# Attention probabilities gated before the transpose, values as stationary weights, modulation rows through DRAM, and channel sums on VectorE, in a decoder layer on one core

## The reference

```python
mod = silu(c) @ w_ada + b_ada                       # six vectors of 1024
h = rmsnorm(x, g_pre_mix) * (1 + sc1) + sh1
q, k_c, k_s, k_w, v_c, v_s, v_w, g_nsa, glu, g_merge = split(h @ w_in)
# 16 heads in 4 groups of 4; q and k 96 wide, v 64 wide
o = g[0] * softmax(q kc') vc + g[1] * softmax(q ks' + bias) vs + g[2] * softmax(q kw' + bias) vw
y_b = silu(layernorm(depthwise_conv31(a * sigmoid(gate)))) @ w_conv_out
y = sigmoid(g_a) * (o @ w_attn_out) + sigmoid(g_b) * y_b
x = x + gt1 * rmsnorm(y @ w_out, g_post_mix)
h = rmsnorm(x, g_pre_ffn) * (1 + sc2) + sh2
# product-key retrieval: 8 heads x top-16 of 16384 experts for each token
x = x + gt2 * rmsnorm(sum_e coef_e * v[e], g_post_ffn)
```

## Time and profile before

| | us |
|---|---|
| Median of 3 runs | 1219.2 |
| Lowest and highest | 1200.63, 1225.37 |
| Profiled execution | 1195.33 |
| Its span, first to last instruction | 1193.6 |
| TensorE matmul busy in the span | 1004.1 (84%) |
| VectorE busy | 728.4 (61%) |
| ScalarE busy | 278.1 (23%) |
| GpSimd busy | 324.7 (27%) |

### The profile page before, as it was taken

How to read it: one execution, slowest core, us unless ns; L and a number is a source line. 1 busy time by engine, 2 the same in 40 slices (tenths; PEclk the granted TensorE clock), 3 DMA queues, 4 the chain that set the end, 5 groups by cost and what they waited for, 6 DMA issues and landing times.

```text
span 1193.6 us, 10994 instructions
## 1 busy us (share of the span) xinstructions
PE 1004.1 (84%) x3386; PEld 617.0 (52%) x3386; DVE 728.4 (61%) x1772; ACT 278.1 (23%) x731; POOL 324.7 (27%) x311
## 2 busy tenths in 40 slices
PE   5899999999999996969888777788777777778676
PEld 5688888787667763845453333333333332333222
DVE  6699895222646313465547676777677767666553
ACT  3111122231535202231212221222132212221211
POOL 0201000010000000224335644444544444445420
PEclk9899999999959998989998989988998989989998
DMA  9977648838000232498788999999999999999992
GB/s 370 403 302 227 245 159 319 298 96 186 1 1 2 92 137 88 155 423 327 303 335 331 425 422 423 423 423 424 422 422 424 423 421 424 422 424 422 422 425 121
DMA packets 62536, 361.37 MB, mean 303 GB/s; under 512 B 7275, under 2 KB 7915, under 8 KB 29452
## 3 DMA queue, kind: packets, MB, share of 16 engines
q0 software_dynamic: 42400, 290.47, 60.4%
q1 hardware_dynamic: 20076, 70.18, 16.7%
HBM read 359.05 MB, written 1.57 MB: 302 GB/s over the span
## 4 chain that ended last, share of the span: by engine, by line
PE 49%; DMA 36%; DVE 5%; ACT 3%; issue 2%; POOL 2%; SPq 2%; POOLq 0%; ACTq 0%; DVEq 0%
DMA arena<-in_peer_uv,idx 33%; PE pb L423 21%; PE pb L649 13%; PE pb L454 4%; PE pb L575 2%; DMA ring<-in_w_stream 2%; PE pb L547 2%; POOL qT L396 2%; DVE arena L1205 1%; PE pb L474 1%; DMA hT<-in_peer_uv,idx 1%; PE pb L558 1%; PE pb L571 1%; ACT sig L845 1%; PE pb L530 1%
## 5 line engine op out<-in xcount | busy, mean ns | idle before, releaser
L649 PE MATMUL pb<-arena,sig 128*128 128x512 f32 x444 | 222.9, 651 | 62.4 <-ACT sig L845 62.4
L396 POOL DMA_INDIRECT arena<-in_peer_uv,idx x111 | 127.1, 1145 | 263.9 <-PE pb L649 137.6
L423 PE MATMUL pb<-hT,ring 128*128 128x256 f32 x880 | 190.7, 379 | 1.2 <-ACT hT L801 0.7
L1205 DVE CUSTOM_DVE_ANT_0 arena<-arena,sig 128x1024 f32<-128x1024 f32 x111 | 135.0, 1227 | 90.5 <-DMA arena<-in_peer_uv,idx 90.1
L649 PEld LDWEIGHTS pb<-arena,sig 128*128 128x128 f32 x444 | 91.2, 210 | 185.4 <-issue 185.4
L423 PEld LDWEIGHTS pb<-hT,ring 128*128 128x128 f32 x880 | 167.0, 190 | 25.2 <-ACT arena L708 1.7
L649 PE MATMUL pb<-ring,sig 128*128 128x512 f32 x208 | 110.0, 689 | 37.0 <-ACT sig L845 37.0
L840 ACT ACTIVATE gl<-dot 128x4 f32<-128x4 f32 x64 | 13.1, 205 | 407.7 <-DVE dot L1205 407.6
L649 PEld LDWEIGHTS pb<-ring,sig 128*128 128x128 f32 x208 | 45.0, 222 | 101.9 <-issue 101.9
L947 DVE SCALAR_TENSOR_TENSOR y<-arena,cols,y x240 | 95.2, 483 | 0.0
L845 ACT ACTIVATE sig<-ident,cf 128x128 f32<-128x128 f32 x256 | 81.8, 390 | 18.3 <-DVE cf L1211 18.3
(11 more groups left out here) (221 smaller groups left out, 1335.7 us busy)
## 6 DMA issues: line engine op xcount, KB each, us to landing
ring<-in_w_stream SPq DMA_DIRECT2D x103, 512.0 KB, 4.7
arena<-in_w_ada POOLq DMA_DIRECT2D x32, 512.0 KB, 9.9
arena<-in_w_ada SPq DMA_DIRECT2D x12, 512.0 KB, 13.1
arena<-in_w1k SPq DMA_DIRECT2D x8, 512.0 KB, 6.0
sig<-in_w_ada SPq DMA_DIRECT2D x4, 512.0 KB, 15.2
arena<-in_w1v POOLq DMA_DIRECT2D x1, 2048.0 KB, 8.1
arena<-rev_scratch POOLq DMA_DIRECT2D x8, 256.0 KB, 11.0
arena<-in_peer_uv,idx POOLq DMA_INDIRECT x111, 25.8
```

The costliest lines, as they stand in the source:

```text
L396: nc.gpsimd.indirect_dma_start(out=rowat[PLACE[n]], out_offset=None, in_=a["peer_uv"], in_offset=bass.IndirectOffsetOnAxis(ap=idx[:, c, e: ...
L423: last = mm(pb[:, bank, 0:SEQ], w[:, k * P:(k + 1) * P], src[:, k, :], start=(k == 0), stop=(k == DT - 1))
L649: last = mm(pb[:, 4 + 2 * t + hf, :], diag[:, c % DEEP, e, :], rowat[PLACE[n]][:, D + hf * 512:D + (hf + 1) * 512], start=(i == 0 and e == ...
L1205: V_.tensor_tensor_reduce(out=u, in0=u, in1=h2[:, c // CPT, :], scale=1.0, scalar=0.0, op0=ALU.mult, op1=ALU.add, accum_out=dot[:, c % DEE ...
```

## The change

1. *Gating.* VectorE multiplies reciprocal sums and gates for each unit (`shares`), and scales the exponentials in `S` before their transposition (`gated`, one `tensor_scalar` for each of two branches); for the compressed branch `cmp_gated` does this once a group. Transposes wait for that. `S` has four buffers now, in `y`'s place.
2. *Values.* `values` is done once a group: V (128 keys x 64) is the stationary operand, the probabilities of four heads (512 columns) the moving one, and all branches accumulate in one bank. The result is transposed already: ScalarE copies it to `hT` (`attention_out`). `combine`, `attn` and its transposes are gone. TensorE, ScalarE and VectorE run their steps in another order (below).
3. *Scores* of the first token tile are computed for its 128 keys only.
4. *Rows.* TensorE transposes `vec4` ahead of the V projections, ScalarE copies it to `vrow`, GpSimd writes it to DRAM, and reads each row back to all partitions by a broadcast DMA, three after the subkeys and one after the last values. `row` and `wide` are gone. `T_OUT` products go tile by tile with the merge (`v_m`), into banks 2 to 5.
5. *Channel sums.* VectorE adds the eight tiles, and TensorE multiplies `ones` once with the sum. The mean stands ahead of the V projections, the variance ahead of the `w1k` block.

Cut to its core:

```diff
         S_ = pair[:, 0:D]
-        S = S_.rearrange("p (u b t) -> p u b t", u=2, b=2)
+        S = yf.rearrange("p (u b t) -> p u b t", u=4, b=2)
         revsb = pair[0:HEADS, 0:512]
-        wide = S_.rearrange("p (j t) -> p j t", j=DT)
         junk = sc[:, 0:1024]
         tmp = pair[:, D:2 * D]
-        PT = tmp.rearrange("p (a b) -> p a b", a=2)
+        PT = arena[:, 8:12, :].rearrange("p a b -> p (a b)").rearrange("p (u k t) -> p u k t", u=2, t=512)
         scaled = [tmp, sc[:, 1024:2048]]
         spare = sb("spare", [P, 2 * D])
-        PcT = spare[:, 0:512]
+        PcT = spare[:, 1024:2048].rearrange("p (u t) -> p u t", u=2)
...
+            g.wait_ge(a_vec, 1)
+            g.dma_start(rows_dram, vrow[:, :]).then_inc(rows_out, 16)
             g.wait_ge(p_hk, 1)
             g.dma_start(w1[:, 0:CMP_ST, :], a["w1v"]).then_inc(w1v_in, 16)
...
             g.dma_start(subk, a["subkeys"]).then_inc(sub_in, 16)
+            g.wait_ge(rows_out, 16)
+            for v in range(4):
+                if v == 3:
+                    g.wait_ge(p_o, GROUPS * TT)
+                g.dma_start(rows[v], rows_dram[v * DT:(v + 1) * DT].rearrange("j p -> (j p)").partition_broadcast(P)
+                            ).then_inc(rows_in, 16)
...
+            pe.wait_ge(v_vec, 4)
+            nc.tensor.transpose(pb[0:4 * DT, 7, 256:256 + P], vec4[:, :, :].rearrange("p v j -> p (v j)"),
+                                ident[:, :]).then_inc(p_vec, 1)
+            pe.wait_ge(v_ys, 1)
+            mm(pb[:, 4, 0:SEQ], ones[:, :], tmp[:, 0:SEQ], start=True, stop=True).then_inc(p_mean, 1)
             pe.wait_ge(a_evac, evacuated(T_V - 1))
             for k in range(DT):
                 token_tile(k, T_V + k, hT, (0, 2), VHALF)
 
 
-            pe.wait_ge(v_y, 2)
-            for k in range(DT):
-                last = mm(pb[:, 4, 0:SEQ], ones[:, :], y[:, k, :], start=(k == 0), stop=(k == DT - 1))
-            last.then_inc(p_mean, 1)
-
+            pe.wait_ge(v_sq, 1)
+            mm(pb[:, 4, SEQ:2 * SEQ], ones[:, :], tmp[:, SEQ:2 * SEQ], start=True, stop=True).then_inc(p_var, 1)
 
             pe.wait_ge(w1_in, 128)
             pe.wait_ge(v_pos, 4)
...
-                pe.wait_ge(a_cexp, gi + 1)
+                pe.wait_ge(v_pc, gi + 1)
...
-                mm(pb[:, n % 2, :], qT[0:DQK, h, tt * P:(tt + 1) * P], kT[0:DQK, g, 1:3, :],
+                mm(pb[:, n % 2, 0:2 * keys], qT[0:DQK, h, tt * P:(tt + 1) * P], kT[0:DQK, g, 1:3, 0:keys],
                    start=True, stop=True).then_inc(p_s, 1)
...
-                pe.wait_ge(a_exp, 2 * (n + 1))
+                pe.wait_ge(v_p, 2 * (n + 1))
...
-            def values(n):
-                tt, h, g, hh, keys = unit_keys(n)
-                gi = n // REP
-                pe.wait_ge(a_pt, n + 1)
+            def values(gi):
+                tt, g = group_of(gi)
                 pe.wait_ge(a_pct, gi + 1)
-                if gi >= 1 and hh % 2 == 0:
-                    pe.wait_ge(v_o, 2 * (gi - 1) + hh // 2 + 1)
-                o = (hh % 2) * 3 * DV
-                bank = 6 + hh // 2
-                mm(pb[:, bank, o:o + DV], PcT[0:NCMP, hh * P:(hh + 1) * P], vcv[:, g * DV:(g + 1) * DV],
-                   start=True, stop=True)
+                pe.wait_ge(a_pt, REP * (gi + 1))
+                if gi >= 2:
+                    pe.wait_ge(a_o, 2 * (gi - 1))
+                o = pb[0:DV, 6 + gi % 2, :]
+                mm(o, vcv[:, g * DV:(g + 1) * DV], PcT[0:NCMP, gi % 2, :], start=True, stop=False)
                 for b in range(2):
                     for kb in range(tt + 1):
-                        last = mm(pb[:, bank, o + (1 + b) * DV:o + (2 + b) * DV],
-                                  PT[:, n % 2, (b * (tt + 1) + kb) * P:(b * (tt + 1) + kb + 1) * P],
-                                  V[:, kb, (b * GROUPS + g) * DV:(b * GROUPS + g + 1) * DV],
-                                  start=(kb == 0), stop=(kb == tt))
+                        last = mm(o, V[:, kb, (b * GROUPS + g) * DV:(b * GROUPS + g + 1) * DV],
+                                  PT[:, gi % 2, b * (tt + 1) + kb, :], start=False, stop=(b == 1 and kb == tt))
                 last.then_inc(p_o, 1)
 
-            for n in range(NU + 2):
+            for n in range(NU + 3):
                 if n < NU:
                     if n % REP == 0:
                         cmp_scores(n // REP)
                     scores(n)
-                    if n % REP == 1:
+                    if n % REP == 2:
                         cmp_transposes(n // REP)
-                if 1 <= n <= NU:
-                    transposes(n - 1)
-                if n >= 2:
-                    values(n - 2)
-
-
-            pe.wait_ge(v_at, 2 * GROUPS * TT)
+                if 2 <= n < NU + 2:
+                    transposes(n - 2)
+                if n >= REP + 2 and (n - 3) % REP == REP - 1:
+                    values((n - 3) // REP)
+
+
             pe.wait_ge(a_pt, NU)
             pe.wait_ge(a_pct, GROUPS * TT)
-            for t in range(TT):
-                for jj in range(2):
-                    for j in range(4):
-                        last = nc.tensor.transpose(pb[:, 2 + 2 * t + jj, j * P:(j + 1) * P],
-                                                   attn[:, t, (4 * jj + j) * P:(4 * jj + j + 1) * P], ident[:, :])
-                    last.then_inc(p_at, 1)
 
             wide_bank = (0, 1, 6, 7)
 
-            pe.wait_ge(a_xT, 4)
-            pe.wait_ge(v_o, 2 * GROUPS * TT)
+            pe.wait_ge(a_o, 2 * GROUPS * TT)
...
-            def row(v):
-                pe.wait_ge(v_row, v + 1)
-                if v >= 2:
-                    pe.wait_ge(a_row, v - 1)
-                for j in range(DT):
-                    last = mm(pb[:, 2 + 2 * (v % 2) + j // 4, (j % 4) * P:(j % 4 + 1) * P], wide[:, j, :], ident[:, :],
-                              start=True, stop=True)
-                last.then_inc(p_row, 1)
-
-            for v in range(2):
-                row(v)
-
-
             for k in range(DT):
-                token_tile(k, T_OUT + k, y, (0, 6), 512)
-            for v in range(2, 4):
-                row(v)
-
+                pe.wait_ge(v_m, k + 1)
+                token_tile(k, T_OUT + k, y, (2, 4), 512)
...
+            act.wait_ge(p_vec, 1)
+            fn(vrow[:, :], pb[0:4 * DT, 7, 256:256 + P], ACT.Copy).then_inc(a_vec, 1)
...
+            def probabilities_out(n):
+                tt, h, g, hh, keys = unit_keys(n)
                 gi = n // REP
-                act.wait_ge(v_mx, n + 1)
+                act.wait_ge(p_t, n + 1)
                 if gi >= 2 and hh == 0:
...
+                fn(PT[:, gi % 2, 0:2 * (tt + 1), hh * P:(hh + 1) * P],
+                   pb[:, 2 + n % 2, 0:2 * P * (tt + 1)].rearrange("p (k t) -> p k t", t=P), ACT.Copy).then_inc(a_pt, 1)
+
+            def attention_out(gi):
+                tt, g = group_of(gi)
+                act.wait_ge(p_o, gi + 1)
+                o = pb[0:DV, 6 + gi % 2, :].rearrange("p (a b t) -> p a b t", b=2, t=P)
+                for odd in range(2):
+                    fn(hT[odd * DV:(odd + 1) * DV, 2 * g:2 * g + 2, tt * P:(tt + 1) * P], o[:, :, odd, :],
+                       ACT.Copy).then_inc(a_o, 1)
+
+            for n in range(NU + 4):
                 gi = n // REP
                 if n < NU:
+                    exps(n)
                     if n % REP == 0:
                         act.wait_ge(v_csub, gi + 1)
                         fn(Sc[:, :, :], Sc[:, :, :], ACT.Exp).then_inc(a_cexp, 1)
-                    exps(n)
...
+                if 2 <= n < NU + 2:
+                    probabilities_out(n - 2)
+                if n < NU and n % REP == 3:
                     act.wait_ge(p_ct, gi + 1)
-                    if gi >= 1:
-                        act.wait_ge(p_o, gi * REP)
-                    fn(PcT[0:NCMP, :], pb[0:NCMP, 5, :], ACT.Copy).then_inc(a_pct, 1)
...
+                    if gi >= 2:
+                        act.wait_ge(p_o, gi - 1)
+                    fn(PcT[0:NCMP, gi % 2, :], pb[0:NCMP, 5, :], ACT.Copy).then_inc(a_pct, 1)
+                if n >= REP + 3 and (n - 4) % REP == REP - 1:
+                    attention_out((n - 4) // REP)
...
+            V_.tensor_reduce(tmp[:, 0:SEQ], y[:, :, :].rearrange("p j t -> p t j"), AX, ALU.add).then_inc(v_ys, 1)
+            dve.wait_ge(p_mean, 1)
+            ch.link(V_.tensor_tensor(y[:, :, :], y[:, :, :],
+                                     pb[:, 4, 0:SEQ].unsqueeze(1).broadcast_to((P, DT, SEQ)), ALU.subtract))
+            ch.link(V_.tensor_tensor(upad[:, :, 0:SEQ], y[:, :, :], y[:, :, :], ALU.mult))
+            V_.tensor_reduce(tmp[:, SEQ:2 * SEQ], upad[:, :, 0:SEQ].rearrange("p j t -> p t j"), AX, ALU.add
+                             ).then_inc(v_sq, 1)
...
+            def shares(n):
+                tt, h, g, hh, keys = unit_keys(n)
+                dve.wait_ge(a_exp, 2 * (n + 1))
+                ch.link(V_.reciprocal(rz[:, n % 2, :], Z[:, n % 2, :]))
```

(76 more changed lines are left out.)

102 lines of the change are left out of this document (22 added, 80 removed).

## The result

The changed kernel has a median of 1214.8 us over 20 runs (1212.3 to 1218.9). The kernel before, over 20 runs, has 1210.7 us (1191.3 to 1231.4). The ratio, taken against those runs of before that lie within 1.5% of its fastest, is 1.012, interval 1.010 to 1.015. A gain of 1.3% was forecast. By this ratio a loss of about that size was measured; by the medians over all 20 runs it is 0.3%, and by the means 3.4 us, which the scatter doesn't tell from nothing. What is as striking: the old kernel's runs scatter by 40 us, the new one's by 7.

A forecast was written before the change was run, and what follows sets the result against it. TensorE was taken to bound attention and nearly all the chain before the first gather, DMA the gathers behind. Gains of 5.2 + 3.7 + 7.0 = 15.9 us (1.3%) gave 1203 us from median 1219.2; range 1182 to 1222.

The forecast's parts named there:

- LayerNorm: Convolution LayerNorm sums: one matmul each for mean and variance instead of 16 records; 5.2 us less, bounds 2.2 and 6.5.
- Rows by DRAM: Rows broadcast by DMA leave the chain after attention: 7.0 us less, bounds 6 and 7.5; the transfers cost nothing.
- Prices: VectorE's operations in an attention step: `gated` 0.35 us for 256 elements, 0.27 for 128; steps 2.35 and 1.7 us.
- The row at single rate, with two scalars: Profile row of 0.413 us for 256 elements; with single rate for `gated`, attention would be some 3 us longer.
- Where the two meet: Attention's queue order: VectorE stands 3.9 or 2.1 us a group while TensorE runs values; groups 14.9 and 10.5 us.
- The stand at the full clock: VectorE's wait for the next scores, once a group in attention: 2.1 us in the first tile, 3.9 in the second.
- Sum at the full clock: All of attention added up without low clock: 106.8 us against 110.5 before, 3.7 less; bounds -12 and +8.
- a rival at 0.19: The clock: one low spell in attention such as before; total -8, 1211 us; chance 0.19.
- The other rival, the low level for all the attention: Slower than before: TensorE at the low clock throughout attention adds 40 us; +23, 1243 us; chance 0.06.
- Its decision point: The low-level-attention rival decides from 60 us at the low level on, each costing 0.28 us.
- The time forecast: Whole kernel: 15.9 us or 1.3% off the profiled execution; the same fraction of the median 1219.2 gives 1203 us.

The follow-up runs named there:

- fillers: Changed kernel plus unread products where TensorE would wait for the scaled exponentials: one a step 1205.2 us, two a step 1193.7 us; changed kernel 1214.8 us.

## Why the forecast was wrong

- *LayerNorm*: forecast 5.2, measured 5.05 us, with the transfer of `w1v` as the next limit. Right. One price in it was off and cost nothing: the reduction of the squares, taken at 2.3 us after a subtraction of that size, took 3.83, but TensorE didn't wait for it.
- *Rows by DRAM*: forecast 7.0, measured 7.05 us. The broadcasts took 7.3 and 3.9 us and nobody waited for them. Right.
- *Prices*: `gated` was taken at 0.35 and 0.27 us and measured 0.345 and 0.278. The Trainium skill's rule of double rate ("VectorE: DVE Perf Modes", "Mode 2×_2P") holds here: `gated` grows by 67 ns for 128 more elements, `logits`, which has a second input, by 267 ns for 256 more (420 and 687). The row at single rate, with two scalars, that spoke against it was not tried again and stays unexplained.
- *Where the two meet*: the mechanism was right, in the place named. The stand at the full clock was close: with fillers in, groups at a clock of 1.00 took 11.0 us for 10.5 and 15.3 for 14.9.
- *The step that failed* is "Sum at the full clock": 106.8 us for attention, where 134.8 was measured. The values' record was put at 0.43 us and took 0.82 on average, 24.7 us over the 64 of them. The same text had found that TensorE would be idle for a third of each group, and that such idle time speaks for the low level, and left both to a rival at 0.19. The other rival, the low level for all the attention, was priced at +40 us and given 0.06; it came to about 0.7 of that: 75 us at the low level x 0.28 = 21 us, of a difference of 28. Its decision point (60 us at the low level) was exceeded, and the kernel was slower, as it said, though by the ratio only. What remains, 7 us, is not settled: part is the 0.5 us a group of the point above, and part may be that the low level falls just on the values, for which 0.28 would be too little (the old kernel's 0.40 would give 30 us).
- The Trainium skill ("TensorE: Matmul & The Clock Gate", Part 1) has the clock released by activity and withdrawn in idleness. The fillers agree: 0.72, 0.82, 0.93 with none, one and two a step. In the old kernel, though, the low level also came while TensorE's records left no gap; that is open.
- *The time forecast*, 1203 us, was too low by 12 only, and that is luck. Between the two profiled runs the forecast had -15.9 us and 19.05 came, 35 us apart: 28 are attention's sum, 2.4 the way from row 0 to the first gather, 2.8 the gather stage, 1.65 the start. But the forecast carried its 1.3% over to a median 24 us above the profiled run of before, whereas the changed kernel's profiled run (1214.5) is close to its median (1214.8). The profile of before was a lucky run, and this hid two thirds of the error.

## What to carry to other kernels

When a change hands work from a full TensorE to another engine, price TensorE's remaining work at both clock levels. If the same sum shows TensorE waiting in each round, give the low level a large chance: here it held for 75 of 135 us. Time saved on TensorE is then no gain. Spread large products over the steps instead of queueing them in one piece in front of what the next engine waits for (19.7 us less of attention here). If gaps remain, unread products in them can pay: here 21 us of 1215 for two per step. And before a forecast is built on one profile, look where that run lies among the others.

## What the runs showed that was not expected

- On one core, with nothing changed, runs scatter by 45 us (1186.5 to 1231.6), with the mean granted clock (correlation -0.96, 35 runs). The median of three runs told 1219, that of 20 told 1211, and those of later sets of 11 to 25 runs 1202 to 1219.
- The clock can fall and rise within a group of 14 us, in such a phase that most of the long products get the low level and the gaps the high one (0.50 at 306 to 308 us, 1.00 at 362 to 364 us with TensorE busy 0.40 of 2).
- Removing half the columns of 16 score products made the kernel slower: by 10 us between the medians, by 5.5 us in the first four groups of the profiles, with the clock at 0.63 instead of 0.89.
